# Two gate tiles of each RWKV pair multiplied in the row of paired tiles, and the pair's chain laid over 32 weight blocks in place of 64

## The reference

```python
h = rmsnorm(x, p['norm_pre'])
proj = h @ p['w_in']
pa, pb, pc, pg = split_cols(proj, (A_COLS, B_COLS, C_COLS, G_COLS))
ya, (c, n, m) = mlstm_branch(pa, p, (c, n, m), segments)
yb, s_h = hgrn_branch(pb, p, lb, s_h, segments)
yc, shift, s_r = rwkv_branch(pc, p, shift, s_r)
ga, gb, gc = split_cols(jax.nn.sigmoid(f32(pg)), G_SIZES)
merged = (ga * (ya.astype(dt) @ p['w_proj_a']) + gb * (yb.astype(dt) @ p['w_proj_b'])
          + gc * (yc.astype(dt) @ p['w_proj_c']))
y = merged.astype(dt) @ p['w_out']
return x + rmsnorm(y, p['norm_post']), (c, n, m, s_h, s_r, shift)
```

## Time and profile before

| | |
|---|---|
| median of 2 runs | 2392.05 us (2391.26 to 2392.84) |
| the profiled execution | 2397.15 us, its span 2395.3 us |
| TensorE busy | 2330.2 us (97%), 19429 matmuls |
| VectorE busy | 1244.1 us (52%) |
| ScalarE busy | 761.7 us (32%) |
| chain that ended last | PE 83%, DVE 8%, issue 4%, ACT 2%, DMA 2% |
| granted TensorE clock, mean | 0.994 |
| DMA | 242.17 MB, 101 GB/s |

### The profile page before, as it was taken

One profiled execution on the slowest core, in us unless ns is written; L12 is line 12 of the kernel. 1 busy time (PEld: TensorE's weight loads), 2 busy tenths in 40 slices (PEclk: granted clock), 3 DMA queues, 4 the chain that ended last, 5 costly groups with the idle time before them and its releaser, 6 DMA issues.

```text
span 2395.3 us, 46302 instructions
## 1 busy us (share of the span) xinstructions
PE 2330.2 (97%) x19429; PEld 2249.1 (94%) x19429; DVE 1244.1 (52%) x1862; ACT 761.7 (32%) x1138; POOL 47.9 (2%) x71
## 2 busy tenths in 40 slices
PE   5999999999999999999999999999999999999998
PEld 5999999999999999999989989988999999999998
DVE  4444433444387765734536527445646654445354
ACT  5311212112133333323323223233323343324443
POOL 0000000000000000000000000000000000000000
PEclk9999999999999999999999999999999999999999
DMA  5232222222223334112112112131212235444465
GB/s 166 72 125 76 70 88 86 79 80 69 81 81 126 122 104 177 54 47 89 59 47 101 46 47 79 47 133 65 94 71 70 88 117 190 151 147 154 156 208 184
DMA packets 59843, 242.17 MB, mean 101 GB/s; under 512 B 8242, under 2 KB 15588, under 8 KB 39524
## 3 DMA queue, kind: packets, MB, share of 16 engines
q1 hardware_dynamic: 59700, 239.97, 29.4%
HBM read 212.13 MB, written 27.81 MB: 100 GB/s over the span
## 4 chain that ended last, share of the span: by engine, by line
PE 83%; DVE 8%; issue 4%; ACT 2%; DMA 2%; SPq 1%; DVEq 0%; POOL 0%; ACTq 0%; POOLq 0%
PE acc L888 53%; PE acc L1404 6%; PE acc L1035 6%; PE branch L1035 3%; PE branch L1129 2%; PE branch L1404 2%; PE branch L1167 2%; DVE scratch L2091 1%; DVE w_lo L1890 1%; ACT w_hi L1451 1%; DMA w_raw<-in_w_stream 1%; PE branch L1122 1%; PE branch L1312 1%; DMA scratch<-in_x_all 1%; DVE scratch L2500 1%
## 5 line engine op out<-in xcount | busy, mean ns | idle before, releaser
L888 PE MATMUL acc<-act_hi,w_hi 128*128 128x320 f32 (+2 forms) x3776 | 1152.5, 305 | 9.2 <-DVE w_lo L1890 7.3
L888 PE MATMUL acc<-act_lo,w_hi 128*128 128x320 f32 (+2 forms) x3776 | 1120.7, 297 | 0.0
L888 PE MATMUL acc<-act_hi,w_lo 128*128 128x320 f32 (+2 forms) x3776 | 1119.9, 297 | 0.0
L888 PEld LDWEIGHTS acc<-act_hi,w_hi 128*128 128x128 f32 x3776 | 713.5, 189 | 25.6 <-DVE w_lo L1890 8.7
L888 PEld LDWEIGHTS acc<-act_lo,w_hi 128*128 128x128 f32 x3776 | 713.8, 189 | 0.7
L888 PEld LDWEIGHTS acc<-act_hi,w_lo 128*128 128x128 f32 x3776 | 713.3, 189 | 0.0
L1890 DVE TENSOR_TENSOR w_lo<-w_raw,w_hi 128x2048 fp32r<-128x2048 f32 x149 | 341.1, 2289 | 384.4 <-ACT w_hi L1451 383.8
L1451 ACT ACTIVATE w_hi<-w_raw 128x2048 fp32r<-128x2048 f32 x149 | 285.7, 1917 | 183.4 <-PE branch L1404 118.9
L1404 PE MATMUL acc<-act_lo,w_hi 128*128 128x288 f32 x384 | 114.0, 297 | 2.8 <-issue 2.8
L1404 PE MATMUL acc<-act_hi,w_lo 128*128 128x288 f32 x384 | 113.7, 296 | 0.0
L1404 PE MATMUL acc<-act_hi,w_hi 128*128 128x288 f32 x384 | 113.6, 296 | 0.0
(11 more groups left out here) (445 smaller groups left out, 2794.8 us busy)
## 6 DMA issues: line engine op xcount, KB each, us to landing
w_raw<-in_w_stream SPq DMA_DIRECT2D x150, 1024.0 KB, 4.9
w_raw<-in_w_stream SPq DMA_DIRECT2D x40, 512.0 KB, 6.4
gate_logits<-gate_out SPq DMA_DIRECT2D x48, 288.0 KB, 2.1
scratch<-gate_logits SPq DMA_DIRECT2D x48, 288.0 KB, 3.1
scratch<-in_x_all SPq DMA_DIRECT2D x9, 512.0 KB, 5.8
branch_rows<-branch_out SPq DMA_DIRECT2D x16, 288.0 KB, 2.2
scratch<-in_x_all SPq DMA_DIRECT2D x3, 1024.0 KB, 10.7
out_y_prompt<-scratch SPq DMA_DIRECT2D x6, 512.0 KB, 2.9
```

What stands on the lines that cost most here:

```text
L888: last = mm(acc[s][:, at:at + hi - lo], a[:, s, w], b[:, k, lo:hi], start=(k == order[0] and a is whi and b is xh), stop=(k == order[-1] a ...
```

## The change

Of the four gate tiles of an RWKV pair, two stay in the pass (N(4) and N(5)); the other two become a pair of the row stage, so there are 14 row pairs in place of 10, and 6 tiles in a pass of the RWKV loop. The plan of the chain is the same list, with each block number halved, over 32 blocks. The evacuations and weight splits of the two tiles leave the lists of ScalarE and VectorE; the high split of the next pass's first tile (N(6) now) comes behind the copies of level 3, its low split stays at the chain's end. Behind the last row pair TensorE waits for c12 where it waited for c21, and VectorE does c12 ahead of the copy of the corner.

```diff
 PLAIN = 4
-N_PAIRS = (N_G - PLAIN) // 2
+N_PAIRS = (N_G - PLAIN) // 2 + NP_C
+C_RUN = C_TILES - 2
...
+def pair_tile(p, m):
+
+    i = p - (N_PAIRS - NP_C)
+    return gate_tile(PLAIN + 2 * p + m) if i < 0 else C_AT + C_TILES * i + C_RUN + m
...
             with looped(sp, 0, NP_C) as i:
-                for j in range(C_TILES):
-                    n = Num(C_N, C_TILES, i, j)
+                for j in range(C_RUN):
+                    n = Num(C_N, C_RUN, i, j)
...
                 row_product(p, "p3", "s4", corner(KHI, THI))
-            pe.wait_ge(*added(N_PAIRS - 1, "c21"))
+            pe.wait_ge(*added(N_PAIRS - 1, "c12"))
...
                 plan += [(block + 1, means), (block + 2, turn_states), (block + 5, variances)]
-                assert block + 5 <= 4 * KT
-                products([N(4), N(5), N(6), N(7)], plan)
+                assert (block + 5) // 2 <= 2 * KT
+                products([N(4), N(5)], [(at // 2, stage) for at, stage in plan])
...
                 other_side(0)
-                act.wait_ge(gates_out[0], i * 32 + 16 * (ROW_STORES))
+                for lv in range(1, 4):
+                    other_side(lv)
+                act.wait_ge(gates_out[0], i * 16 + 16 * ROW_STORES)
                 plain(N(4), gbuf[0][:, :])
                 split_hi(N(6))
-                for lv in range(1, 4):
-                    other_side(lv)
-                act.wait_ge(gates_out[1], i * 32 + 16 * (ROW_STORES))
-                plain(N(5), gbuf[1][:, :])
-                split_hi(N(7))
                 for lv in range(4, LEVELS):
                     other_side(lv)
...
-                    if c == 1:
-                        act.wait_ge(gates_out[0], i * 32 + 16 * (ROW_STORES + 1))
-                        plain(N(6), gbuf[0][:, :])
-                        split_hi(N(8))
...
-                split_hi(N(9))
-                act.wait_ge(gates_out[1], i * 32 + 16 * (ROW_STORES + 1))
-                plain(N(7), gbuf[1][:, :])
+                split_hi(N(7))
+                act.wait_ge(gates_out[1], i * 16 + 16 * ROW_STORES)
+                plain(N(5), gbuf[1][:, :])
...
+                sum_row(p, "p3", gbuf[0][:, TH:KEPT], u5_row, "c12")
                 if top:
                     dve.wait_ge(corner_back[1], 16)
                     v.tensor_copy(xl[:, KLO, THI], saved[1]).then_inc(corner_lo, 1)
-                sum_row(p, "p3", gbuf[0][:, TH:KEPT], u5_row, "c12")
...
                     lower_parts(lv)
-                    if lv == 1:
-                        split_lo(N(6))
...
-                    elif lv == 5:
-                        split_lo(N(7))
```

More of the change, by code:

```diff
@@ L68 @@
 PLAIN = 4
-N_PAIRS = (N_G - PLAIN) // 2
+N_PAIRS = (N_G - PLAIN) // 2 + NP_C
+C_RUN = C_TILES - 2
 SHORT = 2 * N_PAIRS
-C_N, B_N, PROJ_N, OUT_N, AGAIN_N, TILES_N = (n - SHORT for n in (C_AT, B_AT, PROJ_AT, OUT_AT, AGAIN_AT, N_TILES))
+C_N = C_AT - (N_G - PLAIN)
+B_N, PROJ_N, OUT_N, AGAIN_N, TILES_N = (n - SHORT for n in (B_AT, PROJ_AT, OUT_AT, AGAIN_AT, N_TILES))
 def gate_tile(t):
@@ L84, in stream_of, with pair_rows @@
         return A_AT + (n - A_AT) // A_RUN * A_TILES + (n - A_AT) % A_RUN
-    return gate_tile(n - G_AT) if n < C_N else n + SHORT
+    if n < C_N:
+        return gate_tile(n - G_AT)
+    return C_AT + (n - C_N) // C_RUN * C_TILES + (n - C_N) % C_RUN if n < B_N else n + SHORT
+def pair_rows(p):
+    i = p - (N_PAIRS - NP_C)
+    return PLAIN + 2 * p if i < 0 else N_G + C_GATES * i + 2
+def pair_tile(p, m):
+    i = p - (N_PAIRS - NP_C)
+    return gate_tile(PLAIN + 2 * p + m) if i < 0 else C_AT + C_TILES * i + C_RUN + m
 KH, TH = KT // 2, KEPT // 2
 PRODUCTS = 7
-ROW_STORES = N_G // 2
+ROW_STORES = PLAIN // 2 + N_PAIRS
 def row_slot(p, m):
@@ L652, in _, with next_load @@
             sp.dma_start(masks[:, :], masks_in).then_inc(masks_here, 16)
-            def next_load(n, back=0):
+            def next_load(n, back=0, stream=None):
                 nxt = sp.snap(n + 2) if not isinstance(n, int) else n + 2
@@ L661, in next_load @@
                 else:
-                    src = w_stream[bass.ds(sp.snap(nxt + (SHORT - back)), 1)].rearrange("a p n -> (a p) n")
+                    src = w_stream[bass.ds(sp.snap(nxt + (SHORT - back) if stream is None else stream), 1)].rearrange("a p n -> (a p) n")
                 sp.dma_start(wraw[:, s, :], src).then_inc(w_here[s], 16)
@@ L1075, in N @@
                 def N(j):
-                    return Num(C_N, C_TILES, i, j)
+                    return Num(C_N, C_RUN, i, j)
                 def ranks():
```

24 lines of the change are left out of this document (12 added, 12 removed).

## The result

The changed kernel is slower than the forecast by more than its range allowed: 2458.98 us (two executions, 2447.47 and 2470.50) beside 2392.05, a ratio of 1.0284 with a 95% interval of 1.0201 to 1.0367. The forecast was 2427, at most 2445. Its own executions also lie far apart: 23 us in this pair and 25 us over all eight that were taken, against 1.6 us in the pair of the kernel before and at most 7 us in its later series. The profiled execution is the slower one: 2470.50 us, span 2468.6, mean granted clock 0.973.

The account below looks back on a forecast made before the run. TensorE was taken as the limit, with its serial chain with ScalarE already setting the pace in half of a level. Row pairs +90.1 less 54.8 from the RWKV chains gave +35.3 on 2392.05: 2427 us, own range 2414 to 2440.

Parts of the forecast that it names:

- Row pairs: Row stage: four more pairs of 168 matmuls, 22.36 us each, cost 89.4 us, with no new bound.
- The wait for c12: End of the row stage: TensorE waits for VectorE's c12, the sum of the last product; 0.7 us, once.
- The chain at full clock: RWKV stage, one pair's chain from bonus to the end of variances: 90.8 us, from 104.5, over 32 blocks.
- A level: One level of the block inverse in the RWKV chain, join to join: 7.05 us instead of 7.56.
- The walk: RWKV chain summed step by step from trace durations and start distances: 90.8 us changed, 104.6 unchanged.
- the chain fits anyway: Rival: VectorE and ScalarE answer within one block everywhere in the chain, all 101.6 us come back; 2380.5 us, chance 0.06.
- the waits cost more: Rival: 25 to 30 bare waits per RWKV pair cost 0.15 us more each; +16, 2443 us, chance 0.10.
- half-hidden: Rival: TensorE's change of shape around blocks was overcharged, 2 us per pair come back; 2419 us, inside the forecast's range.
- 16.6 us of waits: New RWKV chain: TensorE waits 16.6 us per pair, against 2.7 in the old chain.
- They add nothing to the sum: RWKV chain: idle gaps of at most 1.6 us between blocks do not lower TensorE's clock; no time added.
- The rival of the falling clock: RWKV chain: two half-clock stretches of some 5 us per pair; +20, 2447 us, up to +296; chance 0.06.
- The other edits at no cost: Mid-chain: the remaining weight split (1.91 us) and gate evacuation fit in ScalarE's 3.3 us behind level 3's second copy; free.

Follow-up runs that it names:

- the narrow matmuls: Changed kernel with two 32-column matmuls at each place under the chain's bare waits where another run added one of 288 columns; 2452.69 us, ratio 1.023.
- The wide matmuls: Changed kernel with 62 low-by-low matmuls of 288 columns per pass added under the chain's bare waits; 2427.47 us, ratio 1.0135.

## Why the prediction was wrong

**Row pairs: right.** 89.4 us forecast for four, 91.15 measured for the stage with the wait at its end, 89.46 without. VectorE is busy 199.08 of 289.15 us there, the same share as in the earlier trace rows.

**The wait for c12: right in kind, too small.** 0.7 us forecast, 1.69 measured. c12 itself takes 0.46 (0.45 in the earlier trace rows). TensorE's timeline at the end of the row stage:

```profile
1027.53 0.29 PE L1051 MATMUL acc<-act_hi,w_lo 128*128 128x288 f32 x1
1029.51 0.41 PE L904 MATMUL acc<-act_hi,w_hi 128*128 128x320 f32 x1 [1.69 <-issue]
```

and VectorE's:

```profile
1027.86 0.46 DVE L2100 TENSOR_TENSOR gate_out<-acc,scratch 128x288 f32<-128x288 f32 x1 [0.57 <-PE acc L1051]
```

VectorE has finished at 1028.32, and TensorE starts 1.19 us later, put down to issue: the RWKV loop is entered behind this wait, and the sum had 0.05 for it. Before, where the wait for c21 had long been met, the loop's first matmul started without a gap (940.27, the end of the row stage in the earlier trace rows). That it is the entry of the loop that takes the time fits, but is not shown by a run of its own. The term of the sum was short by 1.0 us, once.

**The chain at full clock: right.** 90.8 us forecast from the earlier trace rows; 90.35 to 90.67 measured wherever the clock held with the same plan, all of them chains with added wide matmuls (30 to 62) that were meant to lie hidden; without any, no whole chain held 1.00, and the nearest, at 0.98, took 91.9. A level 7.05 forecast, 7.03 measured. The walk also gave 101.6 for the 64 blocks laid anew, measured 101.70. So the rivals on the length of the waits (the chain fits anyway, the waits cost more, half-hidden) all fall. The forecast's 16.6 us of waits is not what the profile shows, 10.8 to 11.5 us, but its 2.7 for the old chain is not either (0.5): the two count differently, probably since a wait of the profile begins only at the modelled end of the operation ahead of it, so only the lengths can be held against each other.

**"They add nothing to the sum": the step that failed.** It held each gap of the new chain, at most 1.6 us, against the one idle stretch in the earlier trace rows that had lowered the clock, and 20 us of the old chain at 1.00 against the new one. Both comparisons were of the wrong thing. The gaps were as forecast (the largest 1.43), and the clock fell all the same, so the term that stood at nothing was 40.4 us in the profiled execution, with 113 us at half clock. What had changed was not one gap but the stretch as a whole: TensorE was idle 11 us of a chain for 0.5, in eleven gaps of over 0.4 us, and the joins, transposes and small state matmuls had half as many wide product matmuls between them. The old chain's 1.00 said nothing on such a chain. The prediction had named the signs, a clock below 1 and a period above 150 us; the periods were 161.06, 157.14 and 160.56. The Trainium skill ("TensorE: Matmul & The Clock Gate", the section on a second HAM failure mode) says that micro-idles between groups of matmuls can make the clock go back and forth; the trace agrees, 0.82 in a chain with no gap above 1.43 us. That section names idling alone; the narrow matmuls showed that it isn't the idling alone (0.88 in a chain with TensorE busy 101.28 of 103.00 us). The section on PE-mode transpose says of transposes that they don't count as busy in the same way, which the prediction put more strongly; no run here separates them from other small matmuls.

**The rival of the falling clock: right in mechanism, mis-sized and given too little.** It had 0.06, two stretches of 5 us per pair and 2447 us. Measured: 113 us at half clock in the first trace, 28 a pair for its 10; the chains exceed 90.5 us by 41.7 in sum, 0.37 us for each of these 113 us, where the rival had 0.5: the bare waits don't stretch (0.89 us at both clocks), and the small matmuls take 1.7 times as long and not twice. The execution at 2447.87 us is near its number, with about 53 us at half clock for its 40 and 21 us in the chains for its 20; the median, 2452.88, is 6 us beyond. In the sum for the profiled execution, 2397.15 + 35.3 = 2432.5 was forecast and 2470.5 measured: +40.4 in the chains (403.65 less 4 x 90.8), +1.0 at c12, and -3.4 elsewhere: the row stage starts 1.9 us earlier (740.36 for 742.27), the stretches between the chains are 0.6 shorter in sum, and the one behind the last chain 0.9 (811.71 for 812.59). None of this is work that the change touches.

**The other edits at no cost: held.** The splits and evacuations of ScalarE and VectorE make no wait of their own in the chains at 1.00, which came out at the walk's length.

What stays open: why the falls begin in different places from execution to execution of the same code, and how much of it is the idling and how much the kind of matmul. The wide matmuls took away both at once, and all of the falls in that trace; the narrow ones took away nearly all of the idling and some half of the loss of clock. Which of the chain's small matmuls count against the clock was not told apart.

## What to carry to other kernels

Before taking wide matmuls out from between small ones, ask what is left for TensorE over the whole stretch, not how long the longest gap is: the clock fell here with no gap above 1.43 us, and the small matmuls on the path then took 1.7 times as long. Look at the granted clock in windows of the stretch, and at whether the time spreads between executions; a spread of the times that follows the mean clock (17.8 us per 0.01 here) points to it. Moving work off a latency chain gives back only what its waits can spare, here 14 of 25 us a pair, and where they can spare nothing more it may pay to leave the work in, or even to add some (62 spare matmuls a pass made this kernel 25 us faster; 60 in a dense place made it 23 us slower). Laying the same 64 blocks better against the waits gave 2.8 us a pair at no cost.

## What the runs showed of the hardware

- TensorE's clock fell from 2.4 to 1.2 GHz in a stretch where it was busy 89% of the time (93.23 of 104.76 us), and in another where it was busy 98% (101.28 of 103.00), with many small or narrow matmuls in both. With 62 matmuls of 288 columns more under the waits of the first it held 2.4 GHz (clock 1.00, 87.19 of 90.49 us busy).
- At 1.2 GHz a join of 40 small matmuls takes 2.35 us for 1.35 and five transposes 1.27 to 1.33 for 0.77, so 1.7 times, not twice. A wait of 0.89 us for ScalarE's copy has the same length at both.
- The clock fell in the stretch that was thin, and wide matmuls kept it up in the stretch where they stood: 17.10 us at 0.51 at the end of a chain with no block there, 1.00 with 32 matmuls more in that end; with 60 more ahead of the chain it still fell, and the chains read 0.91 to 0.96.
- The first matmul behind the wait at the entry of a loop starts 1.19 us after the awaited VectorE operation ended, where within the chain it is 0.05 to 0.16.
